# Four adjacent down rows per partition, and each half of the down weights as one transfer

## The reference

```
logits = xt @ w_router + b_router;  top 4 of 32 experts, gates = softmax(top 4)
gu  = xblk @ w_gate_up[e] + b_gate_up[e]          # 1024 -> 2048
act = min(gu[:, :1024], 7) * sigmoid(1.702 * min(gu[:, :1024], 7)) * (clip(gu[:, 1024:], -7, 7) + 1)
y   = act @ w_down[e] + b_down[e]                 # 1024 -> 1024
out[token] += gate * y
```

## Time and profile before

| | us |
|---|---|
| median of three runs | 1183.38 (1183.0 to 1183.73) |
| span of the profiled execution | 1182.6 |
| TensorE matmul busy | 1021.1 (86%) |
| VectorE busy | 294.9 (25%) |
| ScalarE busy | 179.9 (15%) |
| data moved | 464.91 MB, mean 393 GB/s |
| granted TensorE clock over 600 to 1100 us | mostly full, lower for a few us after a long wait |

### The profile page before, as it was taken

The page is one execution under the profiler, slowest core; times in us unless marked ns, Lnnn a source line. Parts: engine busy times, 40 slices in busy tenths (PEclk is TensorE's granted clock), DMA queues, the critical chain, the costliest instruction groups (busy, mean ns, idle before and its releaser), DMA issues.

```text
span 1182.6 us, 21683 instructions
## 1 busy us (share of the span) xinstructions
PE 1021.1 (86%) x8300; PEld 506.5 (43%) x8301; DVE 294.9 (25%) x813; ACT 179.9 (15%) x453; POOL 31.7 (3%) x54
## 2 busy tenths in 40 slices
PE   4999999977886999899979997999799979696966
PEld 4847887433342343334333433343335333333333
DVE  4636664241120121112111211121111211111112
ACT  3213340221110111101110111011111111010002
POOL 1001002110000000000000000000000000000000
PEclk9999999978898999999989998999899989898989
DMA  9899925989999979999999999999999999999996
GB/s 351 324 383 378 338 109 225 423 344 413 424 425 425 422 299 425 425 425 425 425 426 426 426 426 425 426 420 426 426 426 407 426 427 426 425 425 426 426 425 252
DMA packets 61485, 464.91 MB, mean 393 GB/s; under 512 B 5901, under 2 KB 10061, under 8 KB 28569
## 3 DMA queue, kind: packets, MB, share of 16 engines
q1 hardware_dynamic: 60736, 462.47, 94.8%
q0 software_dynamic: 336, 1.07, 0.3%
q10 hardware_dynamic: 392, 1.09, 0.2%
HBM read 462.50 MB, written 2.11 MB: 393 GB/s over the span
## 4 chain that ended last, share of the span: by engine, by line
PE 66%; DMA 21%; DVE 5%; issue 4%; ACT 2%; SPq 1%; POOL 0%; DVEq 0%; ACTq 0%
PE pp L1539 24%; DMA arena<-in_w_down_dram 18%; PE pp L1570 14%; PE pp L1325 5%; PE pp L1503 4%; PE pp L1247 2%; PE pp L1338 2%; PE pp L1257 2%; PE po L1400 2%; PE po L1484 2%; PE pp L1512 2%; DMA gain<-gain_dram 2%; DMA arena<-in_w_ada_dram 1%; PE pp L1518 1%; ACT work L720 1%
## 5 line engine op out<-in xcount | busy, mean ns | idle before, releaser
L1539 PE MATMUL pp<-arena,work 128*32 128x256 f32 (+1 forms) x3840 | 373.9, 445 | 20.1 <-ACT work L720 20.1
L1570 PE MATMUL pp<-arena,work 128*32 128x256 f32 (+1 forms) x1920 | 203.6, 466 | 86.8 <-issue 86.8
L1539 PEld LDWEIGHTS pp<-arena,work 128*32 128x32 f32 (+1 forms) x3840 | 166.7, 117 | 211.1 <-issue 125.9
L1570 PEld LDWEIGHTS pp<-arena,work 128*32 128x32 f32 (+1 forms) x1920 | 83.3, 124 | 188.0 <-issue 169.9
L1091 DVE TENSOR_SCALAR work<-pp 128x128 f32<-128x128 f32 (+1 forms) x74 | 25.0, 338 | 402.6 <-PE pp L1539 402.6
L723 ACT ACTIVATE work<-work 128x128 f32<-128x128 f32 (+1 forms) x74 | 25.9, 350 | 403.0 <-DVE work L1091 403.0
L1085 DVE COPY work<-pp 128x256 f32<-128x256 f32 (+1 forms) x37 | 19.5, 526 | 255.4 <-PE pp L1503 255.4
L1503 PE MATMUL pp<-h_sb,work 128*32 128x256 f32 (+1 forms) x480 | 68.1, 467 | 16.1 <-issue 11.2
L1484 PE MATMUL po<-work 64*128 64x512 f32 x304 | 75.5, 615 | 1.2 <-ACT work L739 1.2
L1325 PE MATMUL pp<-arena 128*128 128x256 f32 x256 | 57.1, 382 | 0.0
L804 DVE SCALAR_TENSOR_TENSOR h_sb<-arena,small,h_sb 128x1024 f32<-128x1024 f32 x38 | 49.5, 1303 | 11.1 <-DMA arena<-in_w_ada_dram 9.9
(11 more groups left out here) (224 smaller groups left out, 621.4 us busy)
## 6 DMA issues: line engine op xcount, KB each, us to landing
arena<-in_w_gate_up_dram SPq DMA_DIRECT2D x128, 2048.0 KB, 29.5
arena<-in_w_down_dram SPq DMA_DIRECT2D x32, 2048.0 KB, 34.4
arena<-in_w_down_dram SPq DMA_DIRECT2D x64, 1024.0 KB, 21.6
arena<-in_w_ada_dram SPq DMA_DIRECT2D x11, 2048.0 KB, 14.4
arena<-in_w_in_dram SPq DMA_DIRECT2D x4, 2048.0 KB, 19.6
arena<-in_w_gate_dram SPq DMA_DIRECT2D x4, 2048.0 KB, 13.3
arena<-in_w_out_dram SPq DMA_DIRECT2D x2, 2048.0 KB, 10.1
arena<-in_w_ada_dram SPq DMA_DIRECT2D x2, 1024.0 KB, 13.1
```

What stands on the lines that cost most here:

```text
L1539: mm = t_.matmul(pp[j * m:(j + 1) * m, UP[hh], 0:w].rearrange("p (s f) -> p s f", s=2), hgT[:, at:at + m], gu_w[slot][:, k, :, r * PAIR:(r ...
L1570: mm = t_.matmul(pp[j * m:(j + 1) * m, UP[0], 0:w], actT[:, at:at + m], wd[:, j * w:(j + 1) * w], start=(n == 0), stop=(n == KD - 1))
```

## The change

`BR` goes from 256 to 512, and `dn_v` takes four rows to a partition. Each half of the down weights of an expert becomes one transfer of 2 MB with runs of 16 KB; the upper half is issued after `s_y`, and `s_dhi_free` is gone. Since the contraction tiles hold other rows of `w_down`, the columns of gate and up that a matmul works on change too: they are taken in pairs with a pair left out between them. In a wide block there are still two halves. In a narrow block both go to one PSUM bank as one part, in matmuls of 512 columns, half as many as before, and VectorE and ScalarE work on 256 columns at once. The bias tile now shares storage with the upper half of `gain2`, so its first loads are issued later in the prologue, and the last gain is read back into a free piece of the arena.

```diff
-BR = 256
+BR = 512
@@ the small tiles
-        gain2 = sb("gain2", [P, D])
+        gain2_bias = sb("gain2_bias", [P, D + BR])
+        gain2 = gain2_bias[:, 0:D]
-        bgu = sb("bgu", [96 + NBR, 2, BR])
-        bm = [bgu[32 * h:32 * h + NMOD, :, :].rearrange("p s f -> p (s f)") for h in range(2)]
+        bgu = gain2_bias[0:96 + NBR, D - BR:D + BR].rearrange("p (s f) -> p s f", s=2)
+        bm = [gain2_bias[32 * h:32 * h + NMOD, D:D + BR] for h in range(2)]
@@ views and loads
-        dn_v = w_down[0].rearrange("e (g p r) n -> e p g (r n)", p=P, r=2)
+        dn_v = w_down[0].rearrange("e (g p r) n -> e p g (r n)", p=P, r=4)
+        def parts_of(m, halves):
+            return (tuple(enumerate(halves)), 1) if m == TB else (((0, halves[1]),), 2)
             def load_dlo(slot, e):
-                sp.dma_start(dlo_w[slot].rearrange("p (g r) d -> p g (r d)", r=2),
-                             dn_v[e, :, 0:2, :]).then_inc(s_dlo[slot], 16)
-            def load_dhi(e, r):
-                sp.dma_start(dhi_w[:, 2 * r:2 * r + 2, :].rearrange("p k d -> p (k d)"),
-                             dn_v[e, :, 2 + r, :]).then_inc(s_dhi[r], 16)
-            load_bgu(0, 0)
-            load_bgu(1, 1)
+                sp.dma_start(dlo_w[slot].rearrange("p k d -> p (k d)"),
+                             dn_v[e, :, 0, :]).then_inc(s_dlo[slot], 16)
+            def load_dhi(e):
+                sp.dma_start(dhi_w.rearrange("p k d -> p (k d)"), dn_v[e, :, 1, :]).then_inc(s_dhi, 16)
...
             for slot, i in ((0, 1), (0, 2), (1, 3)):
                 load_gu(slot, slot, i)
+            sp.wait_ge(s_gspill, 16)
+            load_bgu(0, 0)
+            load_bgu(1, 1)
@@ the loop over the experts
-                    sp.wait_ge(s_dhi_free, total)
-                    load_dhi(last_e, 0)
                     sp.wait_ge(s_y, total)
-                    load_dhi(last_e, 1)
+                    load_dhi(last_e)
@@ TensorE's block
+                def columns_of(j, hh):
+                    return (j, hh) if m == TB else (j // 2, j % 2)
+                def up_of(j, hh):
+                    return pp[j * m:(j + 1) * m, UP[hh], :].rearrange("p (s n c) -> p s n c", s=2, c=2)
+                def pairs(cols, h):
+                    return cols.rearrange("p s (n h c) -> p s h n c", h=2, c=2)[:, :, h, :, :]
...
-                    for hh in range(2):
+                    for hh, _ in parts:
                         for j in range(tiles):
-                            r, cols = half_of(j, hh)
-                            mm = t_.matmul(pp[j * m:(j + 1) * m, UP[hh], 0:w].rearrange("p (s f) -> p s f", s=2),
-                                           hgT[:, at:at + m], gu_w[slot][:, k, :, r * PAIR:(r + 1) * PAIR][:, :, cols],
+                            g, h = columns_of(j, hh)
+                            mm = t_.matmul(up_of(j, hh), hgT[:, at:at + m],
+                                           pairs(gu_w[slot][:, k, :, g * BR:(g + 1) * BR], h),
                                            start=False, stop=(k == KD - 1), skip_group_check=True)
...
-                    if k in (4, 6):
-                        pe.wait_ge(s_dhi[k // 2 - 2], dhi_landed)
-                    if n == 2:
+                    if n == 4:
+                        pe.wait_ge(s_dhi, dhi_landed)
+                    if n == 2 and m == TB:
                         pe.wait_ge(s_aTev, halves[1])
-                    if n == 5:
-                        mm.then_inc(s_dhi_free, 1)
```

More of the change, by code:

```diff
@@ L144, in block_program @@
         x1_back = page(0, TT * D).rearrange("p (t d) -> p t d", t=TT)
+        gain2_back = page(2, D)
         y_out = page(1, TT * D).rearrange("p (t d) -> p t d", t=TT)
@@ L278, in block_program @@
         s_dlo = [sem(f"s_dlo{b}") for b in range(2)]
-        s_dhi = [sem(f"s_dhi{r}") for r in range(2)]
-        s_dhi_free = sem("s_dhi_free")
+        s_dhi = sem("s_dhi")
         s_nblk, s_selg = sem("s_nblk"), sem("s_selg")
@@ L437, in _ @@
             sp.wait_ge(s_lg, TT)
-            for r in range(2):
-                load_dhi(0, r)
+            load_dhi(0)
             sp.wait_ge(s_nblk, 1)
@@ L474, in _ @@
             last_e = sp.snap(dhi_expert, min_val=0, max_val=NEXP - 1)
-            sp.wait_ge(s_dhi_free, total)
-            load_dhi(last_e, 0)
             sp.wait_ge(s_y, total)
-            load_dhi(last_e, 1)
+            load_dhi(last_e)
             sp.dma_start(x1_back, x1_dram[:, :, :]).then_inc(s_x1b, 16)
-            sp.dma_start(gain2[:], gain2_dram[0:1, :].to_broadcast([P, D])).then_inc(s_gback, 16)
+            sp.dma_start(gain2_back, gain2_dram[0:1, :].to_broadcast([P, D])).then_inc(s_gback, 16)
             for t in range(TT):
@@ L1492, in block_of @@
                 q = w // P
-                def half_of(j, hh):
-                    return (2 * j + hh, slice(0, PAIR)) if w > PAIR else (j, slice(hh, PAIR, 2))
+                parts, n_signals = parts_of(m, halves)
+                def columns_of(j, hh):
[4 more added lines that the diff above has]
+                    return cols.rearrange("p s (n h c) -> p s h n c", h=2, c=2)[:, :, h, :, :]
                 pe.wait_ge(s_bgu[slot], landed * 2)
@@ L1508, in block_of @@
                 for j in range(tiles):
-                    for hh in range(2):
-                        rows = bias_rows_of(slot, hh)
-                        r, cols = half_of(j, hh)
-                        t_.matmul(pp[j * m:(j + 1) * m, UP[hh], 0:w].rearrange("p (s f) -> p s f", s=2),
-                                  pick[rows, r, 0:m], bgu[rows, :, cols], start=True, stop=False,
+                    for hh, _ in parts:
+                        g, h = columns_of(j, hh)
+                        rows = bias_rows_of(slot, h)
+                        t_.matmul(up_of(j, hh), pick[rows, g, 0:m], pairs(bgu[rows, :, :], h), start=True, stop=False,
                                   skip_group_check=True)
@@ L1520, in block_of, with turn_part @@
                 mm.then_inc(s_turn, 1)
-                def turn_half(hh):
-                    pe.wait_ge(s_actv, halves[hh])
-                    for i in range(q // 2):
-                        mm = t_.transpose(pp[:, (TOKS, TURN)[hh], i * P:(i + 1) * P], sig[:, hh, i:w // 2:q // 2],
-                                          ident[:])
-                    mm.then_inc(s_aT, 1)
+                def turn_part(hh, n):
+                    pe.wait_ge(s_actv, n)
+                    for i in range(2):
+                        mm = t_.transpose(pp[:, (TOKS, TURN)[hh], i * P:(i + 1) * P], sig[:, hh, i:PAIR:2], ident[:])
+                    mm.then_inc(s_aT, n_signals)
                 pe.wait_ge(s_turned, it)
```

52 lines of the change are left out of this document (27 added, 25 removed).

## The result

The median of four runs is 1203.29 us (1201.04 to 1205.66), against 1183.56 (1183.0 to 1185.07) for the kernel before beside it. The ratio is 1.0157, with an interval of 1.0143 to 1.0171: 1.6% slower. The span of the profiled execution went from 1182.6 to 1201.4 us, +18.8. The direction was forecast, the size was not: 1187.4 was predicted, and 1190.5 was the top of the range.

The account below looks back on a forecast made before the run. The prediction saw two clocks, the DMA queue at its ceiling and TensorE freeing buffers late. Later waits and restarts, less faster down loads, gave +4.0 us: span 1186.6, time 1187.4 us, with an 8-in-10 range of 1180.5 to 1190.5.

Parts of the forecast that it names:

- The mechanism that was likeliest: At the four wide-narrow experts the queue's margin of 2.8 to 3.1 us is used up and it empties; chance 0.48.
- Up to place 10: From the start to the upper half's issue after the ninth expert place, the first wide-narrow one: +4.6 us.
- the gain on seven down loads: Faster down loads before the fourth expert's wait cut its 2.5 us of added lateness to 1.8.
- The restart: Empty queue, from issue to landing: 2.43 us beside the bytes, with 4.93 for a 2 MB load.
- The loops: Repeating stretches of four experts, with the queue emptying once in each: 119.65 us, against 119.5 before.
- The end: Queue full for 244.9 us up to the last upper half's landing; then TensorE sets the finish, +4.0 us.
- Part two, the wait for both MB: TensorE's wait for the upper down half: it goes on 2.5 us later against the queue, with nothing hiding it.
- Part three, the later issue: Upper half issued at `s_y`: an empty queue restarts 0.85 us later after narrow blocks, 1.70 after wide; free otherwise.
- Part four, the length of TensorE's blocks: Narrow block +0.1 us (-0.53 gate and up, +0.41 bias), bounds -0.5 and +0.6; gapped columns cost none, at most 0.2.
- Part one, the packets: Each down load, in 16 KB runs, 0.10 us shorter (5.03 to 4.93), bounds 0.06 and 0.15; 6.2 us over 31 experts.
- the packets' best stretch: A stretch of gate-up loads alone, from which 4.93 us was taken for every 2 MB load.
- Part five and the end: Later bias loads in the prologue cost nothing, at most 1.5 us; TensorE's +4.0 us, not the gain's transfer, sets the finish.

Follow-up runs that it names:

- The exchange of two statements in the kernel after: Kernel after, with the register reads of `next_place` moved ahead of the wait for the upper down half; 1191.57 us, ratio 1.006.
- the joined kernel: Kernel before, with the upper down half as one transfer of 8 KB runs issued at `s_y` and one wait; 1197.12 us, ratio 1.0116.
- the one with the narrow block as one part: Kernel before with the joined upper half, plus narrow blocks as one part in matmuls of 512 adjacent columns; 1201.12 us, ratio 1.0135.

## Why the prediction was wrong

The mechanism that was likeliest is what happened. Its sizes were too small nearly everywhere. Against the forecast's own sum, the 14.8 us that the span is over it (18.8 for 4.0) come in where the rows above place them.

**Up to place 10: +9.6 at the issue (552.72 for 543.09), forecast +4.6.** Place 4's landing is 3.3 later, not 1.8: 0.7 us of lateness is there at place 3's landing already, and 0.7 is the gain on seven down loads, which did not come. The two blocks of the double-wide expert are 1.2 longer, not equal. The restart takes 7.8, not 7.36. From the landing at 439.26 to the one at 498.85 it is 59.6 us, 3.0 more than from 433.70 to 490.30 before, where 2.1 was forecast. The wide-narrow expert is 0.8 longer, not 0.1. That makes 1.5 + 1.2 + 0.4 + 0.9 + 0.7 = 4.7 of 5.0.

**The loops: +7.5 in three, forecast +0.45.** The stretch from the joined issue to the landing that TensorE waits for takes 67.7, 67.4 and 67.6 us, forecast 66.83: 2.2 in sum. From the landing to `s_y` it is 0.4 more in sum. The wide-narrow expert takes 48.9, 48.3 and 50.0, forecast 47.6 at most: 4.5 in sum.

**The end: 2.7.** From 918.79 to the landing at 1166.03 it is 247.2 us, forecast 244.9; the narrow last block and what follows it take the rest.

Sorted by the terms of the sum, the 14.8 us are: loads that got no faster, 5.1 (0.6 of it a later landing at place 13); TensorE's longer blocks, 4.4 (3.2 for the narrow ones of the wide-narrow experts and the last one, 1.2 for the two wide ones of the double-wide expert); five restarts that took longer, 2.1; the low clock at 874 us, 1.7; and a later start, which may be this execution's, 0.7. The rest of 0.8 is spread.

By the steps as the prediction put them:

*Part two, the wait for both MB, had its price right and not what it sets off.* At place 4 and at the last wait it is 2.5 us, as forecast. The new wait at place 3, which the forecast didn't look for, costs nothing. But alone the wait costs 8.3 on the kernel before, where 5 was expected: it makes `s_y` late, and between the landings of places 4 and 30 the queue loses 4.2 us by it. Before, too, `next_place` was covered by the second MB, and the forecast said so. It didn't say what follows: joined, those 1.67 us stand in every cycle in which the queue runs out. The exchange of two statements in the kernel after gives 11.7 us.

*Part three, the later issue,* was forecast at 0.85 and 1.70 us for each restart. Alone it gives +2.9. The restart itself was taken as 2.43 us beside the bytes, from a load of 1 MB. A 2 MB load on the empty queue shows 7.7 to 7.9, so 2.8 to 2.9 beside 4.93. That is not the longer runs: in runs of 8 KB it was 8.2 in the joined kernel and 7.8 in the one with the narrow block as one part, in both behind the double-wide expert. Five restarts make 2.1 of the 14.8 us. The Trainium skill gives about 2.0 us for the fixed part (DMA: Bandwidth & Descriptors, Anatomy of one DMA, there for GpSimd's path). The measurement decides, and it is further from the page than my row was.

*Part four, the length of TensorE's blocks, is the other step that failed, with 4.4 of the 14.8 us.* The forecast had a narrow block at +0.1 and a wide one at nothing. In the narrow block the bias cost what was said (+0.42). The -0.53 for gate and up did not come: with the gaps 64 matmuls of 512 columns take 7.41 to 7.49, and 7.07 without them. The activation, all of it behind the last matmul, leaves TensorE standing 0.5 us before it turns to down. The sum is +0.83, above the bound of +0.6. The wide block's +0.7 is the gapped columns, of which the prediction took none and had 0.2 as the upper bound. The Trainium skill would have let one expect none either: a read that keeps two hits in each 16-byte line runs at full bandwidth (SBUF — State Buffer, in the section Door 1), and pairs of float32 with gaps do that. Here they cost 5%, 13.95 to 14.62, in two kernels.

*Part one, the packets, is the step that failed most: 5.1 of the 14.8 us.* In sum it gave nothing. A lower down half lands 4.89 us after the load before it, where it was 4.97, so 0.08 of the 0.10 is there. But the queue's view of 600 to 1100 us reads as follows for the kernel after.
```profile
q1 hardware_dynamic: 14480, 208.41, 99.0%
```
That is 500 x 0.990 / 208.41 = 2.375 us of busy share for a MB, and before it was 500 x 1.007 / 211.94 = 2.376. With a full queue the last 48 loads took 239.4 us, 4.99 each and not 4.93, and before 239.2. The bias loads take back what the down loads give: without them the same 48 loads take 234.9 us after and 236.2 before. The sum had no term for them; the mean of the row (4.98), which it had worked out itself, holds them, and the packets' best stretch does not.

*The clock.* Of TensorE's wide blocks, three hold a stretch with the granted clock near its lower level, 1.2 of 2.4 GHz. Windows of the kernel after:
```profile
576.00:580.00 4.00, 3.92 (x12) 1.31 (x14) 0.00 (x0) 0.03 (x1) 0.00 (x0) 0.61 1.03 438
819.00:823.00 4.00, 4.00 (x12) 1.23 (x14) 0.00 (x0) 0.00 (x0) 0.00 (x0) 0.57 0.99 422
874.00:878.00 4.00, 4.00 (x12) 1.08 (x12) 0.00 (x0) 0.00 (x0) 0.00 (x0) 0.59 1.01 430
```
Such a block's gate and up takes 16.25 us and not 14.62. The one at 874 lies in a wide-narrow expert and is 1.6 us of the third loop. The kernel before has none of them, but it is not tied to the new layout: the kernel before without the bias loads has two (15.65 us for 13.95), the kernels with the halves split again and with adjacent columns have five each. TensorE was busy ahead of them but for 0.7 us, and I have no cause for it.

*Part five and the end* were right as far as can be told: the prologue costs nothing beyond what executions differ by, and the end is TensorE's.

*How it adds up from the experiments.* The wait (+8.3) and the later issue (+2.9) are the joined kernel's +12.4 within the intervals. Everything but the joining, which is the kernel after with the halves split, costs 4.6 (6.0 by the ratios). The two make 17 (20 by the ratios) and the whole change some 19, so they add up. The narrow block as one part is 2 to 4 of it, and what is left, some 2 us and not told from none, is for the gapped reads, the 16 KB runs and the bias tile. The ledger above is against the forecast, this one against the kernel before: the joining is the larger part of the loss, but the forecast's method has some 7 us for it, and for the rest a gain of some 3, where it costs 4.6. Two things stay open: where the low clock in busy blocks comes from, and what the small bias loads do to the queue.

## What to carry to other kernels

Where one buffer serves all rounds, its transfer is best in parts, each waited for and freed by itself: joining them turns a landing and a release that were hidden into time in which both TensorE and the queue stand. A wait that is new or longer costs nothing where a longer one follows, however it looks in the timeline (4.7 us at place 3, and 0.0 at the next landing). It costs where the engine's lateness next empties the queue, and there everything behind the landing counts, down to two register reads. So follow the landings from round to round before a wait is blamed. A margin can hide a cost in one kernel and not in the next (two register reads: nothing, and 11.7 us), so an edit has to be measured in the kernel in which it is to stand.

## What the runs showed of the hardware

- A moving operand in pairs of float32 with gaps of a pair costs 5% or a little more: 14.62 us for 64 matmuls of 512 columns, side by side in twos, and 13.95 adjacent. Four side by side: 7.41 to 7.49 and 7.07.
- Two loads of 8 KB for each expert among twelve MB cost 8 us in 1184. A full queue loses 0.34 us for an expert by two of them and 0.12 by one, and 0.61 in the kernel after. Issued from ScalarE they cost the kernel as much.
- Runs of 16 KB in place of 8 KB for a third of the bytes took a quarter of the queue's packets away (19553 to 14480 in 500 us) and made a 2 MB load 0.08 us shorter (4.97 to 4.89).
- On an empty queue a 2 MB load lands 7.7 to 7.9 us after its issue in 16 KB runs and 7.8 or 8.2 in 8 KB runs, a 1 MB one after 4.9.
- The granted clock can fall to 0.57 to 0.61 for some 4 us in a block, with TensorE idle for only 0.7 us ahead of it; such a wide block takes 1.6 to 1.7 us longer.
